# Down projection of a SwiGLU layer: 18 of 22 tiles by seven half-size products, activations also stored unsplit

## What is computed

```python
def swiglu(h, w_gu, w_down):
    g, u = jnp.split(h @ w_gu, 2, axis=-1)
    return (jax.nn.silu(g) * u) @ w_down
# in reference, for each layer, prompt and sample alike:
#   x = x + gate * swiglu(modulate(x, norm_ffn, shift, scale), w_gu, w_down)
```

## Time and profile before

| | us |
|---|---|
| median of 3 runs | 2856.87 (2854.5 to 2859.77) |
| the profiled execution, its own time | 2856.11 |
| its span, first to last instruction | 2854.2 |
| PE busy | 2752.9 (96%) |
| DVE / ACT / POOL busy | 1492.7 / 935.1 / 1160.0 |
| DMA | 366.41 MB, mean 128 GB/s |
| granted PE clock, mean | 0.988 of full |

### The profile page before, as it was taken

The page is one execution under the profiler, slowest core; times in us unless marked ns, Lnnn a source line. Parts: engine busy times, 40 slices in busy tenths (PEclk is TensorE's granted clock), DMA queues, the critical chain, the costliest instruction groups (busy, mean ns, idle before and its releaser), DMA issues.

```text
span 2854.2 us, 61199 instructions
## 1 busy us (share of the span) xinstructions
PE 2752.9 (96%) x22137; PEld 2550.0 (89%) x22137; DVE 1492.7 (52%) x2891; ACT 935.1 (33%) x2091; POOL 1160.0 (41%) x1256
## 2 busy tenths in 40 slices
PE   6999999999999999999889999999999999999999
PEld 5898999998999999999787787878789999998998
DVE  4767678665333343423556666666676434335224
ACT  5121212355433443000543233332464444440004
POOL 4000000355555564333754333333376666653324
PEclk8999999999999999999999999999999999999999
DMA  7422111544555535631133524343453333246422
GB/s 260 135 75 92 51 39 38 196 132 135 190 195 191 186 103 196 222 113 43 56 114 102 159 86 148 97 136 109 151 181 117 112 95 118 89 131 244 150 67 82
DMA packets 335403, 366.41 MB, mean 128 GB/s; under 512 B 25188, under 2 KB 272087, under 8 KB 333799
## 3 DMA queue, kind: packets, MB, share of 16 engines
q1 hardware_dynamic: 311282, 327.13, 35.0%
q10 hardware_dynamic: 15732, 28.31, 2.8%
q0 software_dynamic: 8192, 8.40, 1.1%
HBM read 281.95 MB, written 81.82 MB: 127 GB/s over the span
## 4 chain that ended last, share of the span: by engine, by line
PE 87%; DVE 5%; ACT 3%; issue 2%; DMA 1%; POOL 1%; SPq 1%; DVEq 0%; ACTq 0%; POOLq 0%
PE bank L3630 23%; PE bank L3631 22%; PE bank L3632 22%; PE bank L4248 2%; PE bank L4367 2%; PE bank L4269 2%; PE bank L3759 1%; PE bank L4290 1%; PE bank L3921 1%; PE bank L3893 1%; PE bank L4355 1%; DVE xT L2475 1%; PE bank L3938 1%; DMA adae<-in_w_ada 1%; PE bank L4237 1%
## 5 line engine op out<-in xcount | busy, mean ns | idle before, releaser
L3630 PE MATMUL bank<-t_high,op_h 128*128 128x258 f32 x1736 | 496.8, 286 | 8.1 <-DVE t_low L3058 2.8
L3631 PE MATMUL bank<-t_low,op_h 128*128 128x258 f32 x1736 | 492.7, 284 | 0.0
L3632 PE MATMUL bank<-t_high,op_l 128*128 128x258 f32 x1736 | 490.4, 282 | 0.0
L3630 PE MATMUL bank<-hh,whi 128*128 128x344 f32 (+3 forms) x1324 | 439.2, 332 | 29.6 <-DVE ql L3246 7.2
L1271 POOL TENSOR_TENSOR op_l<-raw,op_h 128x512 fp32r<-128x512 f32 x252 | 347.1, 1378 | 282.9 <-ACT op_h L1937 270.9
L3632 PE MATMUL bank<-hh,wlo 128*128 128x344 f32 (+3 forms) x1324 | 422.6, 319 | 0.0
L3631 PE MATMUL bank<-hl,whi 128*128 128x344 f32 (+3 forms) x1324 | 422.2, 319 | 0.0
L3630 PE MATMUL bank<-down_high,whi 128*128 128x344 f32 x1056 | 341.0, 323 | 15.4 <-DVE xT L2475 9.7
L3630 PEld LDWEIGHTS bank<-t_high,op_h 128*128 128x128 f32 x1736 | 328.7, 189 | 21.3 <-issue 16.6
L3631 PE MATMUL bank<-down_low,whi 128*128 128x344 f32 x1056 | 338.0, 320 | 0.0
L3632 PE MATMUL bank<-down_high,wlo 128*128 128x344 f32 x1056 | 337.1, 319 | 0.0
(11 more groups left out here) (496 smaller groups left out, 5816.7 us busy)
## 6 DMA issues: line engine op xcount, KB each, us to landing
raw<-in_w_gu SPq DMA_DIRECT2D x84, 512.0 KB, 4.6
pk<-in_cache_ckv SPq DMA_DIRECT2D x256, 128.0 KB, 2.4
ada_x<-in_w_ada SPq DMA_DIRECT2D x28, 1024.0 KB, 7.1
down_high<-act_high SPq DMA_DIRECT2D x44, 516.0 KB, 5.8
down_low<-act_low SPq DMA_DIRECT2D x44, 516.0 KB, 6.5
act_high<-st_h SPq DMA_DIRECT2D x82, 258.0 KB, 5.0
act_low<-st_l SPq DMA_DIRECT2D x82, 258.0 KB, 5.4
wst<-in_w_in_even SPq DMA_DIRECT2D x28, 512.0 KB
```

Source lines behind the costliest of these rows:

```text
L3630: mm(out, wh_, xh_, start=start, stop=False, skip_group_check=more)
L3631: mm(out, wh_, xl_, start=False, stop=False, skip_group_check=more)
L3632: return mm(out, wl_, xh_, start=False, stop=stop, skip_group_check=more)
```

## The change

**Down by blocks.** Tiles 0 to 17 (in layer 1: 1 to 18) are done in three blocks of six tiles (`DOWN_BLOCKS` = 3). In a block, the six tiles are two halves of `DK` = 3, two neighbouring output tiles are the two row blocks, and the token quarters are the columns. A *Down unit* makes one pair of output tiles from one block: 7 x 2 x 3 x 3 = 126 matmuls of 258 columns. There are 4 pairs x 3 blocks = 12 Down units in a layer, and they follow the gated units without a seam: the same PSUM banks, the same seven products in the same order, the same semaphores. The last four tiles are done as before, one chunk of 4, 288 matmuls of 344 columns in a layer.

**Operands.** Products P1, P2 and P3 use the activations as stored (`block_in` reads the high and low parts from DRAM into `td`, each 3 tiles x 516 columns, 774 KB). P5, P7, P6 and P4 use differences of activations. For them the unsplit activation is now stored too: `store_raw` writes each quarter of `tq` to `act_raw`, and p1_copy and u2_copy of the next unit wait for that store. `stage_load` reads six unsplit tiles back (into xT's space for block 0, otherwise into `stage`), `block_sum` (DVE) forms the differences in place, `block_high` (ACT) and `block_low` (POOL for P5 and P7, DVE for P6 and P4) split them. Each of these handles 3 x 258 = 774 columns at a time, twice per product.

**Results.** No Down unit adds P1..P7 up first: ACT scales P1 and two running sums by the gate factor (`p1_part`, `u2_part`, `u3_part`, which take the place of the copies), and DVE adds each piece to xT (`made_add` from SBUF, `bank_add` from PSUM): 14 additions of 258 columns in a unit. Sample columns are collected in `csum` and added once at the end.

**xT back.** Space for the last stores now lies in xT's tiles 6 and 7, and block 0's unsplit tiles in tiles 0 to 5, so xT comes back in three transfers inside the first Down unit.

The core of the diff:

```diff
-DOWN_CHUNKS = [(0, 2), (2, 4), (6, 6), (12, 6), (18, 4)]
+DK = 3
+DOWN_BLOCKS = 3
+DOWN_UNITS = DOWN_BLOCKS * KT // 2
+LAST_TILES = ([18, 19, 20, 21], [19, 20, 21, 0])
+LAST_N = 4
...
 # PE, product(): the operands of a Down unit
-                for j in range(KH):
+                for j in range(t.half):
...
+                    hi_j, lo_j = (td[p][:, i, j, q, :] for i in range(2)) if t.down else (hi[:, r, b, :], lo[:, r, b, :])
...
 # PE, after the gated units
+                for u in range(DOWN_UNITS):
+                    t = Unit(l, u, None, True)
+                    for p in range(7):
+                        for q in range(2):
+                            if t.starts():
+                                if p in (P1, P2):
+                                    pe.wait_ge(*td_in[0](DOWN_DMA * down_turn(t) + DOWN_DMA))
+                                elif p == P3:
+                                    pe.wait_ge(*td_in[1](DOWN_DMA * down_turn(t) + DOWN_DMA))
+                                else:
+                                    pe.wait_ge(*(td_dve if p in (P6, P4) else td_lo)(down_low(t, p, q)))
+                            product(p, q, t)
...
 # SP, the first Down unit of a layer
+                        sp.dma_start(xT[:, 2 * DK:KT, 0:T], x_rest[:, 2 * DK:KT, 0:T]).then_inc(x_in[1].sem, 16)
+                        sp.wait_ge(*x_in[1](32 * l + 16))
+                        sp.wait_ge(*td_lo(down_low(t, P7, 1)))
+                        sp.dma_start(xT[:, DK:2 * DK, 0:T], x_rest[:, DK:2 * DK, 0:T]).then_inc(x_in[1].sem, 16)
+                        sp.wait_ge(*td_dve(down_low(t, P4, 1)))
+                        sp.dma_start(xT[:, 0:DK, 0:T], x_rest[:, 0:DK, 0:T]).then_inc(x_in[0].sem, 16)
...
 # SP, block_in: a product's region is filled once the last unit of the block before is done with it
+                sp.wait_ge(*block_done[down_after(t, p)](t.count(2, 0)))
+                for i, src in enumerate((act_high, act_low)):
+                    sp.dma_start(td[p][:, i].bitcast(F).rearrange("p k q n -> p (k q) n"),
+                                 src[:, k:k + DK, :].rearrange("p k (q z n) -> p (k q) z n", q=2, z=2)[:, :, there, :]).then_inc(done, 16)
...
 # ACT, in a Down unit
+            def scaled(dst, src, t, m, there, done):
+                gate = mod[:, t.l, 5 * KT + m, 0:1]
+                w = QW - NS if there == 3 else QW
+                ins = nc.scalar.activation(dst[:, 0:w], src[:, 0:w], ACT.Identity, scale=gate)
+                if there == 3:
+                    ins = nc.scalar.copy(dst[:, w:QW], src[:, w:QW])
...
 # DVE, in a Down unit u > 0 (sums: units 1 and 2 of blocks 0 and 1)
+                    p1_add(0, t)
+                    p1_add(1, t)
+                    if t.starts() and u > 0:
+                        block_low(t, P4)
+                    if more and u > 0:
+                        weight_sum(P6, t.next(1))
+                    p2_add(0, t)
+                    p2_add(1, t)
+                    if sums:
+                        block_sum(source, sums[0])
+                    if more and u > 0:
+                        weight_sum(P3, t.next(1))
...
+                    p4_add(0, t)
+                    p4_add(1, t)
+                    if t.ends() and more:
+                        block_low(t.next(1), P6)
+                    p3_add(0, t)
```

609 lines of the change are left out of this document (433 added, 176 removed).

## The result

The changed kernel takes 2882.13 us (median of 5 runs, 2874.22 to 2888.73) against 2856.87 us of the kernel before (5 runs on the same chip): ratio 1.0092, 95% interval 1.0067 to 1.0117. It is slower by 25 us, where 22 us less were forecast. The profiled execution took 2874.22 us, its span is 2872.6 us; the span before was 2854.2 us. So the two traces are 18.4 us apart, and the forecast for that difference was -21.7: 40.1 us have to be found.

A forecast was written before the change was run, and what follows sets the result against it. The prediction took PE, 96% busy, as the bound. Gains of 63.7 us less 4 (sums), 25 (entries), 8 (boundaries) and 5 (exits) left 21.7 us off 2856.1: 2834.4, median 2835 us, range 2812 to 2862.

The forecast's parts named there:

- The columns: PE's Down work: 2592 matmuls of 344 columns removed, 3024 of 258 added at 0.1196 us each, gain 45.2 us.
- Both entries: First two Down units of each layer: late transfers, low parts and block sums cost 13.3 and 11.6 us, together 25.
- ACT's turn: ACT's copies between P6, P7 and P4 in Down units: fits, costed at nothing; as no-change rival 19 us, 2854, 8%.
- The exits: End of each layer's last Down unit: last four tiles' operands late, 2.5 us each, 5 in all (0 to 10).
- Block starts: Four block boundaries: operands 1 us late, ACT and POOL 1 us more; 2 us each, 8 in all (0 to 30).
- The port: Slower rival: POOL holds DVE's two-SBUF-input operations in Down units, 1.9 us in each of 24 units, 46 us, 2880; 13%.
- Units with block sums: Three Down units a layer beside the first: sums before P4's additions cost 0.7 us each, 4 in all (0 to 15).
- The gated part: Gated units store 516 KB more each; the next unit's p1_copy can be some 3 us late; costs nothing.

The follow-up runs named there:

- The version of 2845.90 us: Changed kernel with block sums behind P4's additions, ACT's and DVE's entry orders changed, and store_raw ahead of the weights except in the last gated unit: 2845.90 us, ratio 0.9971.

## Why the prediction was wrong

**What held.** The columns: 1008 matmuls of `td` on each of the three lines, and 15.1 us for a unit's 126 in mid-block, 0.120 us apart. The page's row of the first line, where the earlier trace rows had the 344 columns, and the window of unit 3 of layer 0:

```profile
L4004 PE MATMUL bank<-td,op_h 128*128 128x258 f32 x1008 | 294.9, 293 | 43.7 <-DVE xT L3490 17.9
```

```profile
1186.67:1201.86 15.19, 15.19 (x127) 15.19 (x128) 9.88 (x24) 8.39 (x18) 7.33 (x7) 1.00 0.84 263
```

Both entries: forecast 25 us, measured 27.7. That they are so near is in part luck: PE's waits in the four units are 17.0 us, and 8 more are matmuls at half the clock, of which the forecast knew nothing. The times in it held, with xT's first part landing 17.4 us after the first Down unit's start (17.5 forecast) and the stage at 36.5 (36), where DVE's block sum had waited for it:

```profile
1161.17 2.87 DVE L3462 TENSOR_TENSOR stage<-stage 128x774 f32<-128x774 f32 x2 [6.94 <-DMA stage<-act_raw]
```

ACT's turn: no wait of PE on it in plain units. The exits: forecast 5, measured 7.8, with waits for the last tiles' low parts of 4.3 and 3.1 us.

**Block starts: the term that failed first.** "2 us each, 8 in all" was worked out from the transfers, and "the casts and low parts at the boundary put ACT and POOL behind by nearly all their slack, 1 us more". Measured: 24.6 us, of which 16.3 are four waits on ACT's copy of u behind DVE's list, and 7 the slow matmuls behind them. DVE, which the sentence leaves out, has four low parts of 774 columns there. Their price of 0.96 was right for the instruction alone (0.99) and wrong where it runs (1.77), since POOL works beside it. With POOL's pieces short a start costs 0.1 us, and with these four parts short 1.1 to 2.4. This is 16.6 of the 40.1 us. The transfers, from which I had made the term, were waited for at no boundary of layer 0 in the changed kernel; in the faster versions they were, and at the one boundary that was looked at such a wait was hidden.

The port stood in the prediction as a rival with 13%, at 2880 us, and the time it gave is nearly the one measured. That is luck, since its place was wrong: I let 1.9 us come through in each of 24 units, and the plain units lose nothing. It decides only where all of DVE's and POOL's work for a block comes together. The Trainium skill, page "SBUF — State Buffer", section "SBUF: two separate sides", has the pair as an exclusive lock held for a whole instruction. The traces agree: DVE's part lasts 1.77 and not 0.99 us, one of 24 columns 1.04 and not 0.17, a POOL part of 384 columns 1.7 and not 1.0. Already had shown it at one place. I had cited the rule and then priced the sum without it.

**Units with block sums.** "0.7 us each, 4 us in all": 9.7 measured, and the sums also stood in the way at the entry, in unit 1. "That uses up the slack and a little more" was the right reading; but two of the six additions from SBUF in such a unit last 1.10 and 1.24 us beside POOL (1.11 and 1.23 in unit 2), the others the 0.42 of the earlier trace rows, so the slack was smaller. Moved behind P4's additions the sums cost nothing in units 5 and 6, and 26 us come back in all.

**The gated part.** "The next unit's p1_copy can be late by some 3 us before P6 needs it. Nothing." The copy that was late is the other one, u2_copy, which waits for the store of the second half; SP issues it behind weights. I counted the bytes and not the place in SP's list. It is 2.6 us in layer 0 and 6.0 in layer 1, and with the waits of 1.1 and 1.7 us for the first operands, that no term had either, and their slow matmuls, nearly 12 us. Moving the store took the waits on ACT away, but brought 4.5 us only (4 by the ratios), since the operands' wait grew.

**The clock.** No term had it. The kernel before kept PE at 1.00 through the Down parts, and each of my stalls was counted at its length. Behind the long ones PE then ran 20 matmuls and more at half its clock. Some 16 us of the terms above are of this kind.

**The sum.** Entries 2.7 over, block starts 16.6, sums 5.7, exits 2.8, gated parts and first operands 11.9: 39.7 of the 40.1 us. Two more cancel each other: the last plain tiles, the attention part and the end are 5.4 us longer than forecast, and the profiled execution of the changed kernel reached the first feed-forward part at 645.0 us where the one before came to it at 650.1. No part of the change lies ahead of that point, and the experiments' executions came to it at 645.0 to 651.5: a spread of executions, not an effect.

**What would have made it right.** The version of 2845.90 us keeps the Strassen blocks and beats the kernel before by 0.3% (0.14 to 0.44), some 8 of the 22 us that I forecast. How much of the 37 us of POOL's short parts could be had by an order in which DVE's and POOL's heavy pieces don't meet was not tried.

## What to carry to other kernels

Price a DVE instruction with two SBUF inputs by what runs on POOL in that stretch, not by its fastest row, and add up an engine's list for the half products around a boundary, not for the whole unit: DVE was busy for 15 us on end where I had counted 9 in a unit. If a wait only changes its name when its releaser is moved, that releaser is not the cause; leaving out work on one engine (37 us for POOL's parts, 16.5 for sixteen of DVE's) found it in one experiment each, where orders of ACT and of the transfers only moved it. Keep what can wait (the block sums, 26 us) behind what the next product needs. And where PE has run without a gap, count slow matmuls behind a new one: eight of the nine gaps of 2.2 to 4.4 us in the Down units were followed by them, at 0.4 to 1.2 times the gap each, 15 us behind 28 us of gaps (estimates from the slow stretches and matmuls of the changed kernel's trace).

## What the runs showed of the hardware

- DVE and POOL slow each other both ways: 774 columns on DVE 0.99 us with POOL's pieces short, 1.77 beside its full ones; 384 columns on POOL 1.00 and 1.7. Additions of 258 columns from SBUF went from 0.42 to 1.1 or 1.2 us where they met a piece of POOL.
- A DVE subtraction of 24 columns took 0.17 us at the shortest, 1.04 at the median and 1.59 at the longest beside POOL's parts: shortening DVE's piece doesn't shorten its wait.
- PE's clock was 0.50 behind gaps of 2.66, 3.45 and 4.37 us, and 1.00 behind one of 2.49 us at 1148.46 and those of 1.2 us. Behind 2.23 us at 1139.87 the window of 1140 to 1144 had 0.57. So the length of the gap alone doesn't tell whether the clock falls.
